# Chunks of 64 tokens in the HGRN2 recurrence, with the valid scores copied by predicate into zeroed tiles

## The reference, cut to what matters

```python
cum = jnp.cumsum(gb, axis=2)                       # running sum of log f in the chunk
decay = jnp.exp(jnp.where(causal, rel, -jnp.inf))  # rel = cum[t] - cum[s]
scores = jnp.einsum('bhtk,bhsk,bhtsk->bhts', qb, kb, decay)
o = scores @ vb + (qb * jnp.exp(cum)) @ state
state = jnp.exp(last) * state + (kb * jnp.exp(last - cum)).T @ vb
```

## Time and profile before

| | us |
|---|---|
| median of 3 runs | 961.89 |
| lowest, highest | 961.75, 968.23 |
| the profiled execution, its own time | 962.87 |
| its span, first to last instruction | 961.1 |
| the four prompt tiles of the recurrence, from 352.5 to about 438 in the span | about 86 |

### The profile page before, as it was taken

The page is one execution under the profiler, slowest core; times in us unless marked ns, Lnnn a source line. Parts: engine busy times, 40 slices in busy tenths (PEclk is TensorE's granted clock), DMA queues, the critical chain, the costliest instruction groups (busy, mean ns, idle before and its releaser), DMA issues.

```text
span 961.1 us, 8551 instructions
## 1 busy us (share of the span) xinstructions
PE 739.7 (77%) x3102; PEld 403.9 (42%) x3102; DVE 352.6 (37%) x904; ACT 208.4 (22%) x445; POOL 87.4 (9%) x134
## 2 busy tenths in 40 slices
PE   3799999988889968886689999229678769769600
PEld 1377777634534447774554433113233323223200
DVE  2494836376332352325224534501010111111257
ACT  5311233424433531000020102101010110011132
POOL 1001011201100000000010000321010010110140
PEclk9789999988989965557699999659798899889955
DMA  9772020347422030001495119647999999999462
GB/s 339 234 269 87 1 88 1 130 187 297 147 36 85 3 88 1 1 1 31 124 402 172 44 44 367 197 104 279 422 378 400 422 365 382 419 394 387 163 206 99
DMA packets 50044, 187.24 MB, mean 195 GB/s; under 512 B 12475, under 2 KB 17723, under 8 KB 34134
## 3 DMA queue, kind: packets, MB, share of 16 engines
q1 hardware_dynamic: 32678, 155.39, 41.8%
q10 hardware_dynamic: 10320, 16.10, 5.3%
q0 software_dynamic: 7008, 15.25, 5.1%
HBM read 176.84 MB, written 17.22 MB: 202 GB/s over the span
## 4 chain that ended last, share of the span: by engine, by line
PE 58%; DMA 18%; DVE 10%; ACT 5%; issue 5%; SPq 2%; ACTq 1%; POOL 1%; POOLq 0%; DVEq 0%
PE ps L1533 55%; DMA sb<-in_moe_w_up 12%; DVE sb L929 6%; DMA sb<-in_w_ada 2%; PE ps L1582 2%; ACT sb L709 2%; SPq L348 1%; POOL token_of_row L530 1%; DVE sb L1514 1%; DMA token_of_row<-sb 1%; DVE sb L1526 1%; DMA sb<-y_rows,sb 1%; DMA out_hgrn_sample<-sb 1%; ACTq L792 0%; POOLq L510 0%
## 5 line engine op out<-in xcount | busy, mean ns | idle before, releaser
L1533 PE MATMUL ps<-sb 128*64 128x512 f32 (+9 forms) x2718 | 686.4, 509 | 99.1 <-DMA sb<-in_moe_w_up 49.8
L1533 PEld LDWEIGHTS ps<-sb 128*128 128x128 f32 (+4 forms) x2718 | 355.5, 176 | 397.1 <-issue 326.0
L929 DVE TENSOR_TENSOR sb<-sb 128x16 f32<-128x16 f32 (+18 forms) x368 | 163.3, 484 | 101.3 <-ACT sb L709 46.3
L929 DVE TENSOR_TENSOR sb<-ps,sb 128x256 f32<-128x256 f32 (+6 forms) x69 | 28.9, 440 | 230.1 <-ACT sb L875 188.3
L1582 PE MATMUL ps<-sb 128*128 128x128 f32 (+1 forms) x208 | 31.7, 303 | 37.2 <-DMA sb<-h_rows,sb 33.6
L1582 PEld LDWEIGHTS ps<-sb 128*128 128x128 f32 (+1 forms) x208 | 27.2, 198 | 54.2 <-DMA sb<-h_rows,sb 33.7
L875 ACT ACTIVATE sb<-ps 128x256 f32<-128x256 f32 x16 | 6.1, 383 | 176.9 <-PE ps L1533 176.9
L1236 DVE SCALAR_TENSOR_TENSOR sb<-sb,ps 128x128 f32<-128x128 f32 x60 | 16.8, 342 | 44.6 <-PE ps L1533 44.6
L538 POOL DMA_INDIRECT sb<-h_rows,sb x16 | 16.3, 1017 | 152.9 <-PE ps L1582 150.3
L709 ACT COPY sb<-ps 32x144 f32<-32x144 f32 x64 | 26.2, 410 | 7.4 <-PE ps L1533 5.9
L1500 DVE COPY sb<-ps 128x512 f32<-128x512 f32 x16 | 11.1, 691 | 45.7 <-PE ps L1533 45.7
(11 more groups left out here) (228 smaller groups left out, 351.3 us busy)
## 6 DMA issues: line engine op xcount, KB each, us to landing
sb<-in_moe_w_gate SPq DMA_DIRECT2D x32, 1024.0 KB, 13.6
sb<-in_moe_w_up SPq DMA_DIRECT2D x32, 1024.0 KB, 15.6
sb<-in_moe_w_down SPq DMA_DIRECT2D x32, 1024.0 KB, 8.5
sb<-in_w_ada SPq DMA_DIRECT2D x12, 2048.0 KB, 7.7
sb<-in_w_in SPq DMA_DIRECT2D x5, 2048.0 KB, 10.3
sb<-in_w_ada_final SPq DMA_DIRECT2D x4, 2048.0 KB, 11.1
sb<-in_w_out SPq DMA_DIRECT2D x2, 2048.0 KB, 7.7
sb<-in_x_prompt SPq DMA_DIRECT2D x4, 512.0 KB, 10.1
```

Source lines behind the costliest of these rows:

```text
L929: return dve.tensor_tensor(out, x0, x1, op)
L1533: return pe.matmul(out, lhsT, rhs, start=start, stop=stop, skip_group_check=True)
```

## The change

The constant `CH` goes from 32 to 64, so that the prompt has 8 chunks instead of 16 and a tile 2 instead of 4 (`CPT`). Slices that had 32 written into them follow `CH`. The masked scores of a prompt tile are no longer a product with `maskP`: the two tiles `sT` are zeroed once by VectorE ahead of `mask(0)`, each with a wait for its end (`link`), and from then on `copy_predicated` writes into them only the scores at which `maskP`, read as 32-bit integers, isn't zero. The sample tile keeps the multiplication.

```diff
-    CH = 32
+    CH = 64
     NCH = TP // CH
+    CPT = P // CH
...
-                mk = (maskP if t < PT else maskS).unsqueeze(1).to_broadcast([r, H, r])
-                tt(sT[t % 2][0:r, :, 0:r], ps[2][0:r, :].rearrange("p (h t) -> p h t", h=H)[:, :, 0:r], mk, ALU.mult)\
-                    .then_inc(S["sc_mask"], 1)
+                sc = ps[2][0:r, :].rearrange("p (h t) -> p h t", h=H)[:, :, 0:r]
+                if t < PT:
+                    ins = dve.copy_predicated(sT[t % 2], maskP.bitcast(U32).unsqueeze(1).to_broadcast([P, H, P]), sc)
+                else:
+                    ins = tt(sT[t % 2][0:r, :, 0:r], sc, maskS.unsqueeze(1).to_broadcast([r, H, r]), ALU.mult)
+                ins.then_inc(S["sc_mask"], 1)
...
+            for k in range(2):
+                link(dve.memset(sT[k], 0.0))
             mask(0)
             for t in range(PT):
-                for j in range(4):
-                    c = 4 * t + j
+                for j in range(CPT):
+                    c = CPT * t + j
...
-                    for j in range(4):
-                        c = 4 * t + j
-                        js = slice(32 * j, 32 * j + 32)
+                    for j in range(CPT):
+                        c = CPT * t + j
+                        js = slice(CH * j, CH * j + CH)
...
-                                ins = mm(ob[js, P * h:P * (h + 1)], qT[:, h, t * P + 32 * j:t * P + 32 * j + 32], Sr[c % 3][:, h, :],
+                                ins = mm(ob[js, P * h:P * (h + 1)], qT[:, h, t * P + CH * j:t * P + CH * j + CH], Sr[c % 3][:, h, :],
                                          False, True)
```

## The result

The changed kernel took 929.47 us (median of 4 runs, 924.16 to 933.95) against 965.06 us for the kernel before (4 runs, 961.75 to 969.19). The ratio is 0.9627, 95% interval 0.9553 to 0.9701: 3.7% faster. The profiled execution took 927.40 us (before: 962.87).

What follows compares the result with a forecast made beforehand. TensorE's groups of products, one after another, were taken to bound the prompt's tiles. From 962.9 us, 30.8 off for chunks and 1.0 added for memsets gave 933.1; 6.3 off for the clock gave 927, range 916 to 935.

Steps and rivals of the forecast that it cites:

- Bound: Prompt's tiles: the path runs through TensorE's groups of products one after another; VectorE's state update lies beside the state group.
- Chunks removed: Prompt's tiles: 16 chunks become 8, each removed one a 3.85 us period, so 30.8 us off the path.
- Remaining groups: Update and state groups that stay: pass time unchanged despite wider weights; 1.5 us more if state-group loads lay open.
- The overlap in tile 0: Update groups of chunks 0 and 1 still overlap, as two halves of the rows; 0.8 us lost if they can't.
- Predicated copy: VectorE's masking of scores: copy costs 0.69 us like the multiplication, no change; bounds -0.6 to +2.0 us.
- Zeroed tiles: Two VectorE memsets ahead of `mask(0)`, on the path: about 1.0 us added, bounds 0.6 and 1.8 us.
- The clock: TensorE in the four tiles: rises to 2.4 GHz inside some, 30 of 92 products faster, 6.3 us gained; 0 to 19 possible.
- rises and stays: Rival on TensorE's clock in the loop: 14 to 19 us off, time 914 to 919, say 916; chance 0.17.
- Never inside the chunks: Trace reading before the change: granted clock rose after groups with 128-row weights, never in chunks with 32-row update weights.
- What comes after: Sample tile, state stores and experts' stage move forward with the loop's end, as a whole; 1 or 2 us either way.
- given back: Rival: expert weights' stream starts no earlier, held by something other than the loop; time 962, chance 0.03.
- slower: Rival: VectorE's predicated copy takes a slow element-by-element path, TensorE waiting once a tile; 972 at 10.5 us each, chance 0.02.

Runs made afterwards that it cites:

- three places of the loop: Chunks of 32 and 64 with none, two or four memsets ahead of the loop: 963.8, 950.5, 938.9 us at 32; 917.3, 929.5, 926.8 us at 64.
- the runs with full rows: Update products contract over all 128 rows, state left wrong: kernel before (instead of 32 rows) 935.5 us; changed kernel (instead of 64) 919.91 us.

## Why the prediction was right, and where it was not

The forecast was 927 us with 916 to 935, and the measured 929.47 lies in it. By its steps:

- **Bound.** That the prompt's tiles run through TensorE's groups is right: the loop lost 34.2 us when groups went, and VectorE's update still ends beside the state group.
- **Chunks removed.** 8 x 3.85 = 30.8 us is right at 1.2 GHz, and only there. At 2.4 GHz a chunk of 32 is 2.08 us; over three places of the loop the mean gain is 26.6 us.
- **Remaining groups.** Taken as unchanged; measured 3.90 against 3.85 us for a chunk. Eight loads of 64 columns took 1.56 us where eight of 32 had taken 1.46, and half of that shows in the period. Over the seven chunks with a state group that is 0.3 us, far from the 1.5 us that the prediction gave for loads lying open. The overlap in tile 0 stayed at 2.80 us.
- **Predicated copy.** Taken at 0.69 us, measured 0.72 us. Its loop with the zeroing out of the way is equal to the multiplication's, 42.50 and 42.52 us.
- **Zeroed tiles: the step that failed.** I put them into the sum as about 1.0 us with 1.8 as the upper bound. On the path they are 1.34 us, a third more. But what they do to the time is 10 to 12 us, since the kernels without them run at 919.3 (copies kept) and 917.3. I had named the clock as the uncertain term and yet added the delay to it, as if the clock's pattern didn't depend on where the loop begins. By the runs, a term that moves this loop is also a term of the clock.
- **The clock.** 6.3 us were forecast; the loop shortened by 34.2, which is 3.4 us more than the chunks at 1.2 GHz. So the clock gave about half of its term. That the profiled execution (927.40) came within 1 us of the forecast is luck: the 2.9 us that the loop fell short were made up by its start, 2.0 us earlier by scatter where the sum had it 1.0 us later. The range held by luck of the place too: without the delay the same loop is 8.8 us shorter still, and the time there is that of the rival "rises and stays" (916), although the clock fell twice in that loop as well, at 361.8 and 382.3. The direction, more rows in the weights and so more rises, is what the runs with full rows show at fixed place. "Never inside the chunks, where every second group has 32-row weights" was read rightly from the trace but meant too much: at the next place the same chunks hold 2.4 GHz for 25 us.
- **What comes after.** 523.8 against 523.0 us: moved as a whole, as forecast. The rivals "given back" and "slower" didn't occur.

## What to carry to other kernels

Where a TensorE-bound loop runs at half clock, first look where the clock falls (here only at the pauses of about 2.5 us between tiles) and what keeps it from rising (here weights with few rows), since that can be worth as much as removing products: 29.5 us of loop for full rows, 30.8 us for eight chunks. A single comparison can't price a small edit ahead of such a loop: put a harmless delay in both versions and compare at several places, as a change of 1.3 us here moved the time by 10 to 14 us, one way or the other. And once a copy by predicate costs what the multiplication costs, the chunk's length is free: 128 tokens were better than 64.

## What the runs showed that I had not expected

- A pure delay of 2.6 us on the path made the kernel before 25 us faster (938.88 against 964.44 us).
- TensorE stayed at 1.2 GHz through 41.0 us in which it was busy for 38.5, while the same groups ran at 2.4 GHz elsewhere. Busy time alone does not tell the clock.
- With 32-row updates the clock never rose within a tile's chunks in the kernel before, but once it had risen at 393.2 in the kernel of 32 with predicated copies, it held over two tiles and the pause between them. In these traces it stayed more readily than it rose.
- Twice the loops of two kernels with different instructions but the same place and the same TensorE work agreed to 0.02 us, far better than the times of one kernel's runs, which spread over 3 to 25 us. Read together with the place, the loop's row in the profile was the sharper measure of such an edit here. It comes from one execution, so it says nothing on how the loop scatters.
